# Three reduced-precision passes for the attention scores of a hybrid decoder step, with conversions, silus and side work moved

## What is computed

```
h = rmsnorm(x, norm_g)
qa, ka, va, ga, xb, gb, qc, kc, vc, gc = split(h @ w_in)          # w_in: 1024 x 4608
oa = rmsnorm(retention(qa, ka, va, s0), ret_g)                    # 4 heads of 128
ob = rglru(conv4(xb), h0)                                         # width 512
qc, kc = rmsnorm(qc, q_g), rmsnorm(kc, k_g)                       # 4 query heads, 2 key heads of 128
oc = softmax_with_sink(qc @ kc.T * 128**-0.5 - slope * distance, window 128) @ vc
y = x + concat[oa * silu(ga), ob * silu(gb), oc * silu(gc)] @ w_out
```

## Time and profile before

| | |
|---|---|
| median of 3 runs | 670.89 us (670.74 to 670.92) |
| the profiled execution, its own time | 670.91 us |
| its span, first to last instruction | 668.8 us |
| PE busy | 664.1 us (99%), 5030 matmul records |
| DVE busy | 299.5 us (45%) |
| ACT busy | 290.4 us (43%) |
| POOL busy | 88.7 us (13%) |
| DMA | 54.19 MB, mean 81 GB/s |

### The profile page before, as it was taken

One profiled execution on the slowest core, in us unless ns is written; L12 is line 12 of the kernel. 1 busy time (PEld: TensorE's weight loads), 2 busy tenths in 40 slices (PEclk: granted clock), 3 DMA queues, 4 the chain that ended last, 5 costly groups with the idle time before them and its releaser, 6 DMA issues. The chain is left out here.

```text
span 668.8 us, 12608 instructions
## 1 busy us (share of the span) xinstructions
PE 664.1 (99%) x5030; PEld 647.3 (97%) x5030; DVE 299.5 (45%) x665; ACT 290.4 (43%) x713; POOL 88.7 (13%) x206
## 2 busy tenths in 40 slices
PE   9999999999999999999999999999999999999998
PEld 9999999999999999999999999999999999999998
DVE  6311453453545568686452465237553870400000
ACT  7473343323233377799626555346553450200000
POOL 0001141424342000000012321222100000000000
PEclk9999999999999999999999999999999999999999
DMA  9912105131312301101040202131002441522220
GB/s 342 377 48 96 64 1 203 51 100 32 97 34 64 114 1 63 64 1 64 1 152 6 75 1 80 34 105 64 1 1 87 154 170 36 159 66 66 66 66 32
DMA packets 28149, 54.19 MB, mean 81 GB/s; under 512 B 2520, under 2 KB 20696, under 8 KB 25884
## 3 DMA queue, kind: packets, MB, share of 16 engines
q1 hardware_dynamic: 27804, 52.85, 23.7%
q10 hardware_dynamic: 288, 0.54, 0.2%
HBM read 46.30 MB, written 9.12 MB: 83 GB/s over the span
## 5 line engine op out<-in xcount | busy, mean ns | idle before, releaser
L447 PE MATMUL proj<-big 128*128 128x352 f32 (+1 forms) x912 | 290.1, 318 | 0.0
L449 PE MATMUL proj<-big 128*128 128x352 f32 (+1 forms) x912 | 278.2, 305 | 0.0
L448 PE MATMUL proj<-big 128*128 128x352 f32 (+1 forms) x912 | 278.1, 305 | 0.0
L447 PEld LDWEIGHTS proj<-big 128*128 128x128 f32 x912 | 171.8, 188 | 5.2 <-issue 3.3
L448 PEld LDWEIGHTS proj<-big 128*128 128x128 f32 x912 | 172.0, 189 | 0.2
L449 PEld LDWEIGHTS proj<-big 128*128 128x128 f32 x912 | 172.0, 189 | 0.0
L1249 DVE TENSOR_TENSOR big<-lead,big 128x512 fp32r<-128x512 f32 (+1 forms) x72 | 48.8, 688 | 54.6 <-ACT big L861 54.5
L449 PE MATMUL branch<-m_hi,big 128*128 128x352 f32 x180 | 58.1, 323 | 0.0
L448 PE MATMUL branch<-m_lo,big 128*128 128x352 f32 x180 | 58.0, 322 | 0.0
L447 PE MATMUL branch<-m_hi,big 128*128 128x352 f32 x180 | 58.0, 322 | 0.0
L1709 POOL TENSOR_SCALAR stat<-stat 128x1 f32<-128x1 f32 (+2 forms) x68 | 18.0, 264 | 283.2 <-ACT junk L1023 176.1
(11 more groups left out here) (246 smaller groups left out, 955.3 us busy)
## 6 DMA issues: line engine op xcount, KB each, us to landing
lead<-w_units SPq DMA_DIRECT2D x17, 1024.0 KB, 4.9
xy<-x_T SPq DMA_DIRECT2D x24, 176.0 KB, 2.5
out_y_T<-xy SPq DMA_DIRECT2D x24, 176.0 KB, 1.9
lead<-w_out SPq DMA_DIRECT2D x6, 512.0 KB, 4.0
xy<-w_out SPq DMA_DIRECT2D x6, 512.0 KB, 3.8
mixed<-x_T SPq DMA_DIRECT2D x8, 352.0 KB, 8.0
mixed<-x_prompt SPq DMA_DIRECT2D x5, 512.0 KB, 14.2
s<-state_ret SPq DMA_DIRECT2D x4, 512.0 KB, 4.0
```

What stands on the lines that cost most here:

```text
L447: pe.matmul(out, a_lo, b_hi, start=first, stop=False)
L448: pe.matmul(out, a_hi, b_lo, start=False, stop=False)
L449: return pe.matmul(out, a_hi, b_hi, start=False, stop=last)
```

## The change

- The scores become three float32r passes. `kT` and `qT` hold a high part (index 0, ScalarE's copy) and a low part (index 1). The low parts are new VectorE instructions: `k_low` (128 x 128) and `q_low` (128 x 256), which read the PSUM bank and the high part. The sample tile keeps float32, in tiles of its own (`kT_s`, `q_s`).
- TensorE's turns and scores wait for the low parts too (`kT_low`, `qT_low`). `qT` and `kT` aren't doubled any more: `q_copy` waits for the scores before it, `k_copy` of half 1 for the last scores of half 0.
- In `qC` units the next unit's weights are converted at slots 9, 11, 13, 15 instead of 3, 5, 7, 9.
- Half 1's attention slots from 16 on stand in unit 16 from its slot 0 on; unit 15 has no side work in slots 16 and 17.
- The silus of rows 4 to 7 stand at slots 0, 2, 10, 12 of unit 12 instead of 10, 12, 14, 16.
- At (13, 2) ScalarE does an exponential of one column, so that the function table is loaded there.
- The zeroing of the sample queries (`samp_qzero`) moves from slot 17 to 18 and waits for one more tile of scores.

```diff
+def lows(n9):
+    return NT * (n9 // 9) + min(n9 % 9, NT)
...
-            kT = sb("kT", [P, 2, TOK], scope=r)
+            kT = sb("kT", [P, 2, SEQ], F32R, scope=r)
+            kT_s = sb("kT_s", [P, 2, NS], scope=r)
-            qT = sb("qT", [P, 2, 2 * P], scope=r)
+            qT = sb("qT", [P, 2, 2 * P], F32R, scope=r)
...
-        SILU_AT = {(7, 3): 0, (7, 4): 1, (10, 4): 2, (10, 5): 3, (12, 10): 4, (12, 12): 5, (12, 14): 6, (12, 16): 7}
+        SILU_AT = {(7, 3): 0, (7, 4): 1, (10, 4): 2, (10, 5): 3, (12, 0): 4, (12, 2): 5, (12, 10): 6, (12, 12): 7}
         def w_at(u):
-            return (2, 3, 4, 5) if u == 7 else (0, 1, 2, 3) if 8 <= u <= 11 else (3, 5, 7, 9)
+            return (2, 3, 4, 5) if u == 7 else (0, 1, 2, 3) if 8 <= u <= 11 else \
+                (9, 11, 13, 15) if UNITS[u][0] == "qC" else (3, 5, 7, 9)
         def att_slot(u, s):
-            if u == 13 or u == 15 and s < 17:
+            if u == 13 or u == 15 and s < 16:
...
             if u == 16:
-                return 1, s + 17
+                return 1, s + 16
             if u == 17 and s < 6:
-                return 1, s + 29
+                return 1, s + 28
... (turn_k, TensorE)
                     pe.wait_ge(S_["kT_set"], n9)
+                    pe.wait_ge(S_["kT_low"], lows(n9))
                     if n9 >= 9:
                         pe.wait_ge(S_["qT_set"], 9)
+                        pe.wait_ge(S_["qT_low"], 8)
... (att_q, TensorE)
                 pe.wait_ge(S_["kT_set"], 9 * (n9 // 9) + 9)
+                pe.wait_ge(S_["kT_low"], 8 * (n9 // 9) + 8)
                 if n9 > 0:
                     pe.wait_ge(S_["qT_set"], n9)
+                    pe.wait_ge(S_["qT_low"], lows(n9))
... (att_scores, TensorE)
                 pe.wait_ge(S_["qT_set"], 9 * half + t + 1)
+                pe.wait_ge(S_["qT_low"], n8 + 1)
                 if n8 > 0:
                     pe.wait_ge(S_["biased"], n8)
+                lo = P if t == 0 else 0
                 for g in range(2):
-                    lo = P if t == 0 else 0
-                    mm = pe.matmul(bb[1][:, g * 2 * P + lo:(g + 1) * 2 * P],
-                                   qT[:, (9 * half + t) % 2, g * P:(g + 1) * P],
-                                   kT[:, half, (t - 1) * P + lo:(t + 1) * P], start=(g == 0), stop=True,
-                                   skip_group_check=True)
+                    for i, (a, b) in enumerate(((1, 0), (0, 1), (0, 0))):
+                        mm = pe.matmul(bb[1][:, g * 2 * P + lo:(g + 1) * 2 * P], qT[:, a, g * P:(g + 1) * P],
+                                       kT[:, b, (t - 1) * P + lo:(t + 1) * P], start=(g == 0 and i == 0),
+                                       stop=(i == 2), skip_group_check=True)
... (side, ScalarE)
+                if (u, s) == (13, 2):
+                    act.activation(sp_t[:, 0, 0:1], ones[:, 0:1], ACT.Exp)
... (VectorE)
+            def k_low(n9):
+                half, t = divmod(n9, 9)
+                dve.wait_ge(S_["kT_set"], n9 + 1)
+                if t < NT:
+                    dve.tensor_tensor(kT[:, 1, chunk_cols(t)], bb[0][:, 0:P], kT[:, 0, chunk_cols(t)].bitcast(F32),
+                                      ALU.subtract).then_inc(S_["kT_low"], 1)
+
+            def q_low(n9):
+                dve.wait_ge(S_["qT_set"], n9 + 1)
+                dve.tensor_tensor(qT[:, 1, :], bb[0][:, 0:2 * P], qT[:, 0, :].bitcast(F32),
+                                  ALU.subtract).then_inc(S_["qT_low"], 1)
... (att_side, VectorE, after att_probs, att_mix and att_max)
-                if s == 17:
+                if s == 18:
                     samp_qzero(half)
+                if s % 2 == 0 and 0 <= (s - 2) // 2 < NT:
+                    q_low(9 * half + (s - 2) // 2)
... (side, VectorE)
+                if UNITS[u][0] == "kvC" and s % 2 == 1 and 3 <= s < 17:
+                    k_low(9 * UNITS[u][1] + (s - 3) // 2)
+                if UNITS[u][0] == "qC" and s < 2:
+                    k_low(9 * UNITS[u][1] + NT - 1 + s)
```

More of the change, by code:

```diff
@@ L219, in layer @@
             p_sel = kcT[:, 0:2, :].rearrange("p a n -> p (a n)")
+        with ExitStack() as r:
+            sb("mixed_d", [P, 3 * H, TOK], scope=r)
+            sb("under_q", [P, 2 * TOK + 2 * (NT + 1) * DH + N_CC + 4 * DH + 2 * DH], scope=r)
+            q_s = sb("q_s", [P, 2 * P], scope=r)
         with ExitStack() as r:
@@ L243, in layer @@
             lru_set xb_set a2_set tails_turned tails_copied
-            k_ss k_pow kn_set kT_done kT_set q_ss q_pow qn_half qn_set qT_done qT_set
+            k_ss k_pow kn_set kT_done kT_set kT_low q_ss q_pow qn_half qn_set qT_done qT_set qT_low
             sc_done biased sink_set mx_set ex_set pr_set pT_done pT_set av_done mix_c
@@ L726, in samp_scores @@
                         b = 2 * c + e
-                        q = qT[:, (9 * half + NT) % 2, NS * b:NS * b + NS]
+                        q = q_s[:, NS * b:NS * b + NS]
                         pe.matmul(bb[4][32 * c:32 * c + 32, 0:P], q, kcT[:, b, :], start=(e == 0), stop=(e == 1),
@@ L732, in samp_scores @@
                         b = 2 * c + e
-                        q = qT[:, (9 * half + NT) % 2, NS * b:NS * b + NS]
-                        mm = pe.matmul(bb[4][32 * c:32 * c + 32, P:P + NS], q, kT[:, half, SEQ:TOK], start=False,
+                        q = q_s[:, NS * b:NS * b + NS]
+                        mm = pe.matmul(bb[4][32 * c:32 * c + 32, P:P + NS], q, kT_s[:, half, :], start=False,
                                        stop=(e == 1), skip_group_check=True)
@@ L1031, in k_copy @@
                 act.wait_ge(S_["kT_done"], n9 + 1)
-                act.activation(kT[:, half, chunk_cols(t)], bb[0][:, 0:n], ACT.Copy).then_inc(S_["kT_set"], 1)
+                if half == 1 and t < NT:
+                    act.wait_ge(S_["sc_done"], NT)
+                out = kT[:, 0, chunk_cols(t)] if t < NT else kT_s[:, half, :]
+                act.activation(out, bb[0][:, 0:n], ACT.Copy).then_inc(S_["kT_set"], 1)
             def q_stat(u, j):
@@ L1051, in q_copy @@
                 act.wait_ge(S_["qT_done"], n9 + 1)
[L1052 to L1057, removed]
+                if n9 == 9:
+                    act.wait_ge(S_["ss_done"], 1)
+                elif n9 > 0:
+                    act.wait_ge(S_["sc_done"], lows(n9))
                 if n9 % 9 == NT:
                     act.wait_ge(S_["q_zero"], n9 // 9 + 1)
-                    q = qT[:, n9 % 2, :].rearrange("p (c x) -> p c x", c=4)
+                    q = q_s[:].rearrange("p (c x) -> p c x", c=4)
                     for g in range(2):
@@ L1066, in q_copy @@
                     return
-                act.activation(qT[:, n9 % 2, 0:2 * n], bb[0][:, 0:2 * n], ACT.Copy).then_inc(S_["qT_set"], 1)
+                act.activation(qT[:, 0, 0:2 * n], bb[0][:, 0:2 * n], ACT.Copy).then_inc(S_["qT_set"], 1)
             def att_exp(half, t):
@@ L1569, in samp_qzero @@
             def samp_qzero(half):
-                dve.wait_ge(S_["sc_done"], 8 * half + 7)
-                dve.memset(qT[:, (9 * half + NT) % 2, :], 0.0).then_inc(S_["q_zero"], 1)
+                dve.wait_ge(S_["sc_done"], 8 * half + 8)
+                dve.memset(q_s[:], 0.0).then_inc(S_["q_zero"], 1)
             def samp_probs(half):
```

## The result

| | before | changed kernel |
|---|---|---|
| median of 6 runs | 670.90 us (670.74 to 671.07) | 674.68 us (673.19 to 675.61) |
| the profiled execution | 670.91 us | 674.66 us |
| its span | 668.8 us | 672.5 us |

The ratio is 1.0058, with a 95% interval of 1.0047 to 1.0069: the change makes the kernel 0.6% slower. The forecast was 674.6. The total is met to 0.1 us, but not by the sum that stood behind it: one term of 1.8 us was really 0.5, and a mechanism that I had put among the rivals came in for 1.3 us.

What follows compares the result with a forecast made beforehand. TensorE, busy 99% of the span, was taken as the bound, so only its work or waits count. Terms -2.1 + 1.8 - 0.2 + 0.4 + 0.2 + 3.6 = +3.7 us on 670.91 gave 674.6 us, range 672.4 to 677.4.

Steps and rivals of the forecast that it cites:

- The gap: Border of units 15 and 16: TensorE idles until the fourth weight piece's `w_low`, behind `q_norm(7)`, is done; +3.6 us.
- The clock: Rival, chance 0.14: 3.6 us of idleness before unit 16 halves TensorE's rate for 5.5 us, losing 2.7 us; 677.3 us.
- The blocks of 128 columns: Two t = 0 score blocks: six float32r matmuls each replace two float32 ones; +1.8 us, between -0.1 and +1.8.
- the dear end: Scores of t = 0: each 128-column float32r matmul costs float32's 0.23 us, 1.38 a block, a loss of 0.92.
- The cheap bound: Scores of t = 0: 0.07 us a matmul, 0.40 a block, gain 0.06; as rival 672.8 us, chance 0.27.
- The scores of 256 columns: Fourteen score blocks: six float32r matmuls at 0.12 us, 0.72 instead of 0.87 a block; -2.1 us.
- Silus and the keys' low parts: Key tile 7's border: half 0 loses a 0.61 us wait, `k_low(7)` adds 0.19 in each half; -0.2 us.
- The queries' low parts: Scores wait for `q_low`, late on VectorE behind probabilities and maximum, at slots 6 to 10; +0.4 us, between 0 and 1.2.
- Unit 13 into 14: TensorE waits for the last weight piece, released at 403.22, with `sample_rows`, values, scores and turns as cover; +0.2 us.
- the price of leaving conversions and table load in place: Slot 6: with both left where they were, it would wait about 1 us more for the query low part.

## Why the prediction came out right, and where it wasn't

- **The gap (+3.6).** Right in size, place and cause: 3.67 us, on `w_low` behind `q_norm(7)`. Two experiments that undo one part each show that the conversions set its length and that the side work left it empty. Moving the side work makes no gap by itself: with unit 16's weights converted early it stays moved, and the gap is gone.
- **The clock.** Put among the rivals at 0.14, with 2.7 us; it did fall, in five of six runs, and cost 1.33 us. The mechanism was right, the size was off, and so was my weighing: the forecast and this rival don't exclude each other, and I had given the forecast the gap without its consequence. The size came from the start of the kernel, where the low level lasted 5.5 us; behind this gap it lasted 3 us (472.45 to 475.45).
- **The blocks of 128 columns (+1.8).** This is the step that failed. I took the dear end, float32's 0.23 us a matmul, as the nearest row by shape; the matmuls took 0.11, the blocks lost 0.24 and 0.22, in sum 0.5. The cheap bound was too cheap too: the line through 352 and 256 columns gave 0.07, but there is a floor at 0.11. These two errors, 1.3 too much here and 1.3 missing at the clock, cancelled; that the total was met so closely is luck. The Trainium skill (TensorE: Matmul & The Clock Gate, Back-to-back issue gap) gives about 81 ns for each matmul of 128 columns in a stream of weight loads and matmuls, and names no type there. That is nearer than both my ends, but over a quarter below the 0.11 us measured here for float32r.
- **The scores of 256 columns (-2.1).** Right: 1.73 to 1.57 us a block, 14 x 0.16 = 2.2.
- **Silus and the keys' low parts (-0.2).** Right: -0.48 and +0.25 for -0.4 and +0.2. That ScalarE's silu was the cause is shown by putting it back (+0.77), and that the copies of the sample rows made the rest by moving them (-0.24 and -0.26).
- **The queries' low parts (+0.4).** The sum is 0.6, but not where I put it. Six blocks of half 0 gained 0.90 where 0.96 were due and five of half 1 0.71 where 0.80 were due, so the slots 6 to 10 cost 0.15 in all. The rest is one wait that I didn't have: at the start of unit 14.
- **Unit 13 into 14 (+0.2).** The wait for the weights is there, 0.16 us (the first matmul starts 0.30 us after the turn instead of 0.14). I had left out what the same `w_low` does to the work behind it on VectorE. It pushes probabilities, mix and maximum back, then `q_low(7)`, and the scores of tile 7 wait 0.46 us for that:

```profile
401.41 0.68 DVE L1267 TENSOR_TENSOR big<-lead,big 128x512 fp32r<-128x512 f32 x1
...
404.39 0.41 DVE L1518 TENSOR_TENSOR qT<-branch,qT 128x256 fp32r<-128x256 f32 x1
```

TensorE:

```profile
404.91 0.95 PE L707 MATMUL branch<-kT,qT 128*128 128x256 f32 x6 [0.21 <-issue]
```

The experiments bear this out: from the turn of queries 7 to that of 8 in half 0 the changed kernel takes 5.81 us, and the kernels with the fourth piece of unit 14's weights at slot 13 or earlier take 5.19 to 5.22.

- **What the supporting moves buy.** I had put the price of leaving conversions and table load in place at 1 us for slot 6 of half 0; it is 1.05 (5.15 against 4.10), of which about half is the table load (0.52 when it alone is taken out) and half the conversions. In half 1 it is 0.57. The moves save about 1.6 us there and 0.4 at slot 16 of unit 15. The fourth piece at slot 15, with the side work gone from behind it, costs 5.6 (3.67, 1.33, 0.16 and 0.46).

In the order of the forecast's sum, with the clock behind it, the measured terms are -2.24 + 0.46 - 0.23 + 0.61 + 0.16 + 3.67 + 1.33 = +3.76 us, against +3.71 between the last matmuls.

## What to carry to other kernels

When a conversion or a load is moved later in a hand-made schedule, look where its last piece stands in the queue of each engine that makes it: a piece behind an operation that waits for the end of a stage is late for the start of the next one, and only other work of TensorE can cover that (here 0.16 us of waiting where `sample_rows` stood in between, 3.67 where nothing did). A gap in TensorE's stream can cost more than its length (here 3.67 us and 1.33 for the clock), so price the two together; even filling it with useless matmuls gives something back (1.7 us here). Measure what a small matmul costs before you price it: neither the line through larger ones (0.07 us) nor the same shape in another type (0.23) was near the 0.11.

## What the runs showed of the hardware

- A float32r matmul with 128 weight columns of its own has a pitch of 0.16 us at 352 columns, 0.12 at 256 and 0.11 at 192, 128 and 64. Why it stops falling isn't shown.
- TensorE's granted clock fell at gaps of 3.67 us (five of six runs) and of 2.85 us (one trace, with the clock still full until the matmuls began again), and not where 1.9 us of work stood inside a wait of 3.8 us and left 1.1 us empty. A run of the kernel with the silus back came 2.3 us late (672.31) and kept a mean granted clock of 1.000; it has no trace. Behind the gap of 3.7 us the low level, 0.293 us for 352 columns, lasted 3.0 us.
- At the start of the kernel the matmuls ran at the same low pitch while the granted clock shows full; in the middle of the kernel the page's clock does show the fall (0.59 from 472.4 to 476).
- A three-pass float32r product of 256 columns is cheaper than one float32 matmul (0.36 against 0.43 us), one of 128 columns is dearer (0.31 to 0.34 against 0.22).
